# Differential attention heads: value products and norm sums in float32r halves, with the work of a head put in another order

## What is computed

```python
def diff_attention(x, w_qkv, w_o, lq1, lk1, lq2, lk2, subln_g, lambda_init):
    qkv = x @ w_qkv                      # 8 heads, two 64-wide q/k parts, v of 128
    q = apply_partial_rope(q, cos, sin) * (HEAD_DIM ** -0.5)
    k = apply_partial_rope(k, cos, sin)
    s = jnp.where(mask, jnp.einsum('bqhcd,bkhcd->bhcqk', q, k), -jnp.inf)
    p = jax.nn.softmax(s, axis=-1)
    a = p[:, :, 0] - lam * p[:, :, 1]
    o = jnp.einsum('bhqk,bkhe->bqhe', a, v)
    o = rmsnorm(o, subln_g) * (1.0 - lambda_init)
    return o.reshape(B, S, V_WIDTH) @ w_o
```

## Time and profile before

| | us |
|---|---|
| runs | 2322.46, 2322.62, 2324.59 |
| median | 2322.62 |
| profiled execution, its own time | 2322.65 |
| its span | 2320.9 |
| PE busy | 2300.4 (99%) |
| DVE busy | 1278.9 (55%) |
| ACT busy | 816.7 (35%) |
| POOL busy | 96.5 (4%) |

### The profile page before, as it was taken

How to read it: one execution, slowest core, us unless ns; L and a number is a source line. 1 busy time by engine, 2 the same in 40 slices (tenths; PEclk the granted TensorE clock), 3 DMA queues, 4 the chain that set the end, 5 groups by cost and what they waited for, 6 DMA issues and landing times.

```text
span 2320.9 us, 28961 instructions
## 1 busy us (share of the span) xinstructions
PE 2300.4 (99%) x10614; PEld 1841.6 (79%) x10614; DVE 1278.9 (55%) x1662; ACT 816.7 (35%) x1113; POOL 96.5 (4%) x82
## 2 busy tenths in 40 slices
PE   9999999999999999999999999999999999999999
PEld 8877888888865788888887777888887887888886
DVE  5453643444688644444547867454456655654553
ACT  5376532322413532322424544222224223322222
POOL 0000000000000000000003311000001001000002
PEclk9999999999999999999999999999999999999999
DMA  5210332332553233333332112332332322333331
GB/s 199 82 48 26 109 99 91 99 100 91 186 158 105 73 100 100 98 95 97 108 100 64 55 45 74 109 100 91 99 96 71 113 92 73 109 94 96 99 95 51
DMA packets 64791, 220.05 MB, mean 95 GB/s; under 512 B 8576, under 2 KB 8960, under 8 KB 64448
## 3 DMA queue, kind: packets, MB, share of 16 engines
q1 hardware_dynamic: 64704, 218.85, 30.2%
HBM read 208.62 MB, written 2.10 MB: 91 GB/s over the span
## 4 chain that ended last, share of the span: by engine, by line
PE 94%; DVE 2%; ACT 2%; issue 1%; DMA 0%; POOL 0%; SPq 0%; DVEq 0%; ACTq 0%; POOLq 0%
PE ps L1605 87%; PE ps L2005 2%; PE ps L2098 1%; PE ps L2124 1%; PE ps L1871 1%; PE ps L2114 0%; PE ps L2103 0%; PE ps L1886 0%; DVE spl L1009 0%; ACT sph L532 0%; PE ps L2131 0%; PE ps L1851 0%; PE ps L1665 0%; DVE m L870 0%; DVE sp L1004 0%
## 5 line engine op out<-in xcount | busy, mean ns | idle before, releaser
L1605 PE MATMUL ps<-xh,whi 128*128 128x512 f32 x1764 | 697.9, 396 | 1.4 <-DVE xl L845 0.8
L1605 PE MATMUL ps<-xh,wlo 128*128 128x512 f32 x1764 | 687.1, 390 | 0.0
L1605 PE MATMUL ps<-xl,whi 128*128 128x512 f32 x1764 | 686.7, 389 | 0.0
L839 DVE TENSOR_TENSOR wlo<-raw,whi 128x1024 fp32r<-128x1024 f32 x380 | 473.7, 1247 | 242.9 <-ACT whi L368 233.5
L368 ACT ACTIVATE whi<-raw 128x1024 fp32r<-128x1024 f32 x380 | 398.8, 1050 | 495.4 <-PE ps L1605 492.8
L1605 PE MATMUL ps<-yh,whi 128*128 128x512 f32 x1116 | 437.0, 392 | 1.2 <-DVE m L1375 0.8
L1605 PE MATMUL ps<-yh,wlo 128*128 128x512 f32 x1116 | 434.4, 389 | 0.0
L1605 PE MATMUL ps<-yl,whi 128*128 128x512 f32 x1116 | 434.2, 389 | 0.0
L1605 PEld LDWEIGHTS ps<-xh,whi 128*128 128x128 f32 x1764 | 331.4, 188 | 80.7 <-issue 7.1
L1605 PEld LDWEIGHTS ps<-xl,whi 128*128 128x128 f32 x1764 | 331.3, 188 | 71.5 <-issue 4.5
L1605 PEld LDWEIGHTS ps<-xh,wlo 128*128 128x128 f32 x1764 | 331.1, 188 | 69.8
(11 more groups left out here) (250 smaller groups left out, 1831.2 us busy)
## 6 DMA issues: line engine op xcount, KB each, us to landing
raw<-stream SPq DMA_DIRECT2D x380, 512.0 KB, 3.5
u<-ub SPq DMA_DIRECT2D x118, 67.0 KB, 2.4
tapw<-taps SPq DMA_DIRECT2D x1, 3584.0 KB, 12.1
h<-x_t SPq DMA_DIRECT2D x8, 256.0 KB, 6.0
raw<-stream SPq DMA_DIRECT2D x8, 256.0 KB, 6.2
out_t<-h SPq DMA_DIRECT2D x8, 256.0 KB, 2.3
const<-consts SPq DMA_DIRECT2D x1, 1089.0 KB, 9.0
vec<-vecs SPq DMA_DIRECT2D x1, 180.0 KB, 10.2
```

Source lines behind the costliest of these rows:

```text
L839: dve.tensor_tensor(wlo[:, a.slot], raw[:, a.slot], whi[:, a.slot].bitcast(F32), ALU.subtract)\
L1605: mm = pe.matmul(out, lhs, rhs, start=first and n == 0, stop=last and n == 2)
```

## The change

- v is split: ACT rounds v into vh, POOL stores vl; for the last head both go into block 7 of yh and yl. The transposed weights are split as well: ACT writes the high half into aT, DVE the low half straight from bank 6 (`turned_lo`). `values` then runs once for a head, after all four transposes, in 12 float32r passes of 512, 384, 256 and 128 columns, three of each, where it was 10 float32 matmuls (20 records).
- Bank 6 is free for the next transposes when `turned_lo` has read it (da_al), no longer when ACT has copied it (da_aT).
- The square is split too (ACT into sums 0, DVE `square_lo` into sums 1), and `norm_sum` becomes two float32r passes.
- PE issues the next head's first scores right behind the last transposes and ahead of `values`; `norm_sum` moves behind the next four blocks.
- The scaling by lambda moves from DVE to ACT (`scale`). DVE folds the norm into the tables once (sinq, sin, cos: three operations ahead of the first rotation) and `rope` is two operations, both reading the bank, where it was three. The k tile's rope moves into the following head, behind `inverse(e, 1)`; that of the last k tile stands in head 6.
- In head 6 and 7, `out_lo` stands behind the second `turned_lo`, `split_lo(T_DO + 1)` later than it did, and the last `values(1)` behind three output units.
- The table load at the head of each pair goes (4 loads). Outside the attention, semaphores are merged and nothing is moved on an engine; the copy `exact` has 768 columns, not 640.

The core of the diff: ACT, DVE, POOL, PE.

```diff
+                def scale(e, u):
+                    n, p, kv = 4 * e + u, u % 2, (u + 1) * P
+                    act.wait_ge(s("da_r1"), i * 8 + (n + 1))
+                    act.activation(A["ex"][:, p, 1, 0:kv], A["ex"][:, p, 1, 0:kv], ACT.Copy, scale=A["r1"][:, p])\
+                       .then_inc(s("da_t"), 1)
...
-                def out_square(e):
-                    act.wait_ge(s("da_o"), i * 2 + (e + 1) + CREDIT)
...
+                def stage(e):
+
+                    act.wait_ge(s("da_o"), i * 2 + e + CREDIT)
+                    act.wait_ge(evac_done, T_DA)
+                    act.activation(A["vh"][:], A["dv"][:, :, bass.ds(i * 256 + e * 128, P)], ACT.Copy).then_inc(s("da_vhh"), 1)
+
+                def stage_last():
+
+                    act.wait_ge(s("da_qn"), 2 * DA_HEADS + CREDIT)
+                    act.activation(yh[:, KB - 1].rearrange("p (t c) -> p t c", t=TB), A["dv"][:, :, D - P:D], ACT.Copy)\
+                       .then_inc(s("da_vhh"), 1)
+
+                def out_square(done):
+
+                    act.wait_ge(s("da_o"), done + CREDIT)
                     act.activation(sq[:, 0], ps[:, 7], ACT.Square).then_inc(s("da_sq"), 1)
+                    act.wait_ge(s("da_sq"), done)
+                    act.activation(sums[:, 0], sq[:, 0], ACT.Copy).then_inc(s("da_sqh"), 1)
...
-                act.preload_act_table_set(LN_EXP)
                 for e in (0, 1):
+                    last = e or before
                     exps(e, 0)
-                    if e or before:
+                    scale(e, 0)
+                    if last:
+                        out_square(i * 2 + e)
+                    exps(e, 1)
+                    if fill or e == 0:
+                        stage(e)
+                    if last:
                         out_rms(i * 2 + e)
...
                     copy_T(e, 0)
-                    if e or before:
+                    scale(e, 1)
+                    exps(e, 2)
+                    if last:
                         out_hi(i * 2 + e, i * 2 + (e - 1))
-                    exps(e, 2)
+                    if not fill and e == 0:
+                        stage_last()
+                    scale(e, 2)
...
                     exps(e, 3)
+                    scale(e, 3)
                     copy_T(e, 2)
                     copy_T(e, 3)
-                    out_square(e)
```

```diff
                 dve.wait_ge(tile_done, t.count)
                 if not isinstance(done, int) or done > 2:
                     dve.wait_ge(s("da_qn"), done - 2 + CREDIT)
-                dve.scalar_tensor_tensor(A["draw"][:, c], ps[:, c], 1.0 if c else 64 ** -0.5, rrow[:], ALU.mult,
-                                         ALU.mult).then_inc(evac_done, 1)
-                dve.wait_ge(s("lam_ready"), 2)
-                dve.wait_ge(evac_done, t.count)
-                dve.stream_shuffle(A["dsh"][:, c], A["draw"][:, c], swap).then_inc(s("da_sh"), 1)
-                dve.wait_ge(s("da_sh"), done)
-                dve.tensor_tensor(A["dsh"][:, c], A["dsh"][:, c], cst("sin"), ALU.mult).then_inc(s("da_shs"), 1)
+                straight, crossed = drow[:, c], dcross[:, c]
+                dve.wait_ge(s("da_trig"), 3)
+                dve.scalar_tensor_tensor(straight, ps[:, c], 1.0 if c else 64 ** -0.5, cst("cos"), ALU.mult, ALU.mult)
+                dve.wait_ge(s("lam_ready"), 1)
+                dve.stream_shuffle(crossed, ps[:, c], swap).then_inc(evac_done, 1)
                 if split:
                     split_lo(t)
 
...
-                def combine(e, u):
-
-                    n, p, kv = 4 * e + u, u % 2, (u + 1) * P
-                    done = i * 8 + (n + 1)
+                def inverse(e, u):
+
+                    n, p = 4 * e + u, u % 2
                     dve.wait_ge(s("da_exp"), i * 16 + 2 * (n + 1) + CREDIT)
                     dve.reciprocal(A["rc"][:, p], A["sm"][:, p]).then_inc(s("da_rcp"), 1)
-                    dve.wait_ge(s("da_rcp"), done)
+                    dve.wait_ge(s("da_rcp"), i * 8 + (n + 1))
                     dve.tensor_tensor(A["r1"][:, p], A["rc"][:, p, 1:2], nlam[:], ALU.mult).then_inc(s("da_r1"), 1)
-                    dve.wait_ge(s("da_r1"), done)
-                    dve.tensor_scalar(acc[:, 0:kv], A["ex"][:, p, 1, 0:kv], A["r1"][:, p], None, ALU.mult)\
-                       .then_inc(s("da_t"), 1)
-                    dve.wait_ge(s("da_t"), done)
+
+                def combine(e, u):
+
+                    n, p, kv = 4 * e + u, u % 2, (u + 1) * P
+                    dve.wait_ge(s("da_t"), i * 8 + (n + 1))
                     if u >= 2:
                         dve.wait_ge(s("da_T"), i * 8 + (n - 1))
                     dve.scalar_tensor_tensor(A["da"][:, p, 0:kv], A["ex"][:, p, 0, 0:kv], A["rc"][:, p, 0:1],
-                                             acc[:, 0:kv], ALU.mult, ALU.add).then_inc(s("da_a"), 1)
+                                             A["ex"][:, p, 1, 0:kv], ALU.mult, ALU.add).then_inc(s("da_a"), 1)
+
+                def turned_lo(e, u):
+
+                    dve.wait_ge(s("da_aT"), i * 8 + (4 * e + u + 1))
+                    dve.tensor_tensor(turned(1, u), turned_in(u), turned(0, u).bitcast(F32), ALU.subtract)\
+                       .then_inc(s("da_al"), 1)
...
+                def square_lo(done):
+
+                    dve.wait_ge(s("da_sqh"), done)
+                    dve.tensor_tensor(sums[:, 1], sq[:, 0], sums[:, 0].bitcast(F32), ALU.subtract).then_inc(s("da_sql"), 1)
+
                 for e in (0, 1):
+                    last = e or before
+                    filled = fill and last or e == 0 and before
                     row_max(e, 0)
                     row_max(e, 1)
+                    if filled:
+                        split_lo(Tile(T_DA + 3 + 2 * e, i))
+                    inverse(e, 0)
+                    if last:
+                        square_lo(i * 2 + e)
                     combine(e, 0)
-                    if e or before:
+                    inverse(e, 1)
+                    if filled:
+                        rope(1, Tile(T_DA + 3 + 2 * e, i), i * 4 + (2 * e + 4), False)
+                    row_max(e, 2)
+                    if last:
                         out(i * 2 + e)
-                    row_max(e, 2)
-                    if e or before:
-                        out_lo(i * 2 + e, i * 2 + (e - 1))
                     combine(e, 1)
+                    turned_lo(e, 0)
                     if not fill and e:
-                        split_lo(Tile(T_DO + 1))
                         early_sum(2)
-                    combine(e, 2)
+                    inverse(e, 2)
                     if fill:
                         rope(0, Tile(T_DA + 4 + 2 * e, i), i * 4 + (4 + 2 * e + 1), False)
                     row_max(e, 3)
+                    combine(e, 2)
+                    turned_lo(e, 1)
+                    if last:
+                        out_lo(i * 2 + e, i * 2 + (e - 1))
                     if not fill:
                         early_sum(3 * e)
+                    inverse(e, 3)
                     combine(e, 3)
+                    turned_lo(e, 2)
                     if fill:
                         split_lo(Tile(T_DA + 4 + 2 * e, i))
-                        rope(1, Tile(T_DA + 4 + 2 * e + 1, i), i * 4 + (4 + 2 * e + 2))
-                    elif e == 0:
+                    elif e:
+                        split_lo(Tile(T_DO + 1))
+                    if not fill and e == 0:
                         early_sum(1)
+                    turned_lo(e, 3)
+                    if not fill and e == 0:
                         split_lo(Tile(T_DO))
                 if not fill:
                     split_lo(Tile(T_DO + 2))
                     early_sum(4)
                     split_lo(Tile(T_DO + 3))
+                    square_lo(DA_HEADS)
                     early_sum(5)
                     out(DA_HEADS)
                     out_lo(DA_HEADS, DA_HEADS - 1)
```

```diff
+            def pair_work(pair):
                 for e in (0, 1):
+                    stage(pair, e)
                     rotated(pair, e, 0)
                     rotated(pair, e, 1)
-                    stage(pair, e)
-
-            pair_inputs(0)
-            with pool.Fori(1, 4) as pair:
-                pair_inputs(pair)
+
+            for e in (0, 1):
+                rotated(0, e, 0, 0)
+                rotated(0, e, 1, 0)
+            pair_work(0)
+            with pool.Fori(1, 3) as pair:
+                pair_work(pair)
+            stage(3, 0)
+            stage(3, 1, True)
```

```diff
                 def transposes(e, u):
                     n = 4 * e + u
                     pe.wait_ge(s("da_a"), i * 8 + (n + 1))
-                    pe.wait_ge(s("da_aT"), i * 8 + n + CREDIT)
+                    pe.wait_ge(s("da_al"), i * 8 + n + CREDIT)
...
-                def values(e, u):
-                    n, at = 4 * e + u, P * u * (u + 1) // 2
-                    pe.wait_ge(s("da_aT"), i * 8 + (n + 1) + CREDIT)
```

(50 more changed lines are left out.)

134 lines of the change are left out of this document (78 added, 56 removed).

## The result

The changed kernel takes 2327.45 us (median, 2326.01 to 2329.03), the kernel before 2323.18 on the same chips. The ratio is 1.0019, with a 95% interval of 1.0013 to 1.0024. So the change costs 4.3 us, where 3.2 us of gain were forecast, and the time lies outside the range. From the first scores to the sum behind the output projection the changed kernel takes 1413.75 - 1226.54 = 187.2 us, 182.9 before and 179.7 by the forecast. The whole loss is in this stretch.

What follows compares the result with a forecast made beforehand. PE was taken to bound the kernel (94% of the last-ending chain). Gains of 5.4, 3.7 and 2.7 make 11.8 us, less 8.6 of new waits leaves 3.2: 2322.65 to 2319.4 us, range 2316.0 to 2322.6.

Steps and rivals of the forecast that it cites:

- PE's own prices: Values from 2.61 to 1.94 us a head, norm sum from 0.92 to 0.46; over eight heads 5.4 and 3.7 us gained.
- The door: Start of head 6: the first output unit waits for the last k tile's rope, PE stands 4.8 us, bounds 4 and 5.5.
- Wait 2: Norm sum in heads with filling tiles: its chain is level with PE's work, 0 taken, up to 1.5 us.
- The wait on yl: Units 10 and 11 of head 6 need head 5's yl from the later out_lo; PE stands 1.3 us.
- the early sum: Head 6, behind the units waiting on yl: PE stands 0.2 us for the sum of the same bank.
- wait 5: Two norm sums at the end: 0.7 us of waiting in head 7 and 0.2 behind it.
- The wait ahead of the values: Each of seven heads: PE waits 0.2 us for the split of the last transposes, 1.4 us in all.
- waits that go: Exponentials in head 0 (0.9 us), an early sum in the last pair (0.8), last transposes in seven heads (1.0): 2.7 us gained.
- rival C: The norm sum's chain is late everywhere; with 1.5 us a head the time is 2328.4; chance 0.07, milder form 0.1.
- rival B: PE comes back at half rate behind head 6's 4.8 us stall, losing 2.3 us, time 2321.7; chance 0.23.
- Rival A: Head 6's wait for the last tile falls away or is short: gain 8.0 us, time 2314.6; chance 0.12.

Runs made afterwards that it cites:

- e1: Changed kernel with the first output unit of head 6 waiting for one tile fewer, not the last k tile; 2321.01 us, ratio 0.9990.
- e10: e5 with the norm sum as one float32 matmul of the square again; 2318.72 us, ratio 0.9982 to the kernel before.
- e5: Changed kernel with head 6's first output unit waiting one tile fewer, v's low half between rotations, out_lo behind third turned_lo in filling heads; 2315.87 us.
- e2: Changed kernel with POOL's rotation operations and low half of v beside the heads cut to 8 columns, for times alone; 2323.01 us, ratio 0.9998.
- e9: Changed kernel with PE running 19 more passes into empty bank 0 while it waits for the last k tile in head 6; 2325.61 us, ratio 1.0011.
- e6: Changed kernel with the scaling by lambda back from ACT to DVE, ahead of each combine; 2334.23 us, ratio 1.0047.
- e4: Changed kernel with POOL doing v's low half between the two rotations of a head instead of ahead of both; 2324.82 us, ratio 1.0008.

## Why the prediction was wrong

**What held.** PE's own prices: the values from start to start 1.98 (e1's rows, 1344.93 to 1346.91) for a forecast of 1.94, a gain of 0.63 for 0.67; the norm sum two passes of 0.23, in e10 against e5 worth 0.40 for 0.46. The door: 4.43 us of idle time, 4.6 by the starts (the distance of two starts, less the pass between them), for 4.8, at the place and for the reason that was walked through. The profile puts this wait down to "issue" and not to DVE's shuffle, but the shuffle of the last k tile runs from 1349.48 to 1350.20, PE starts at 1350.30, and e1 takes the wait away by that tile's count alone. Wait 2 on the norm sum in the heads with filling tiles, called the soft place: no wait at all, as taken. The wait on yl 1.14 of idle time, 1.31 by the starts, for 1.3; the early sum 0.20, 0.37 by the starts, for 0.2; wait 5 in head 7 0.41 for 0.7. The wait ahead of the values: from the masks to the values the starts lie 0.62 and 0.82 apart in turn, where the masks alone take 0.50, so 0.12 and 0.32 for 0.2 in each.

**What failed: "waits that go", the last transposes.** I wrote that the combine gets one block more and credited 0.15 for each of seven heads. In its place the transposes wait 0.6 to 0.75 us in heads 1 to 5, which eats nearly all that PE saves there. The credit itself was there to take in those five heads only: in heads 0 and 6 of the kernel before the last transposes start 0.24 and 0.23 behind the pass, with no wait. The sum asked for the path of DVE only at four places (values, norm sum, door, yl) and here it didn't: `transposes(e, 3)` now waits for `turned_lo(2)`, which on DVE stands behind `combine(e, 3)`, and that behind everything from the third row maximum on. With DVE at its usual durations that is just in time (e2: no wait). But DVE loses some 2.2 us a head to POOL, 0.8 at the combine, 0.5 at r, 0.75 at `out_lo` by the starts of the next operations and 0.15 at the larger combine. On PE that comes to 19.80 - 18.95 = 0.85 a head, 4.3 us in five.

The sign of it stood in the forecast's own rows. The earlier trace rows has `split_lo` at 1.77 beside POOL and 1.22 without; I used this as a bound for one chain and in rival C, and against C set that POOL should be idle "then". The question should have been asked for every DVE operation with two inputs in SBUF, since the change moves those: in the heads of the kernel before, POOL's rows lie beside shuffles, row maxima and `split_lo`, and the combines, the product with lambda and `out_lo` run while POOL is idle. The Trainium skill, "SBUF — State Buffer", section "Who interferes with whom", says that a DVE instruction with two SBUF inputs contends with a GpSimd instruction that reads SBUF, and that whichever comes first keeps the shared ports for its whole length; one with at most one such input doesn't contend unless it runs in a 2-port mode. By that rule three of DVE's operations in each head are held until POOL's operation ends, and the rows of the changed kernel and e2 agree, down to the product of one column that took 0.83 us and ended within 0.01 us of POOL's vl. It was a rule that spoke against this change, and the forecast didn't weigh it.

**What was priced, but not chosen: rival B.** The forecast gave 0.23 to PE coming back at half rate behind the door, at 2.3 us. It did, at 1.7 us in the changed kernel (e9 gives 1.55 in the trace, 1.8 by the medians). The Trainium skill, "TensorE: Matmul & The Clock Gate", Part 1, whose rule stood beside this rival, agrees with this trace: the granted clock fell behind a stall of 4.4 us in the middle of the program. It stayed at 1.00 around the wait of 1.14 (e5, 1351 to 1359), and the passes behind the waits of 0.75 come at the full rate. One reading of the earlier trace rows has to be taken with care: the profile lists a granted clock of 1.00 for 1.46 to 6.10 us as well, so there only the durations speak for 1.2 GHz, while behind the door clock and distances agree.

**Rival C** named a slower kernel by DVE's lateness, but at the wrong wait: no row waits on the norm sum in heads 1 to 5. Its price, five or six times the lateness of a head, and its reason, POOL, were close, though the `split_lo` that it named keeps its 1.22 (head 5, 1324.74). Rival A was false as it stood, and e1 made it true by one number.

**The balance.** The stretch missed by 7.5 us. Heads 1 to 5 account for 4.8: 4.3 for POOL's hold, the rest for gains of 0.63 and 0.40 instead of 0.67 and 0.46. The clock behind the door is 1.7. Head 0 is 0.5 above its part, 0.24 of it a wait for its first combine and 0.15 the credit for a wait that wasn't there. Head 6 has 24.9 us by the forecast's terms (19.72 before, less 0.67, 0.46 and 0.15, plus 0.2, 4.8 and 1.5) and took 26.93: beyond the clock 0.3 more, as the door gives back 0.2, the start behind each of the two waits on output units costs 0.1, the early sum 0.2 more by its starts, and the credit 0.15. Behind head 6 only 0.2 is missed: the sum at the end waits 0.48 for acc (L1625), which no step had, and the waits on the norm sums, 0.41 for 0.9, give it back.

## What to carry to other kernels

When an edit makes the bounding engine faster, every engine close behind it must be walked through at each wait, not only at the waits that the edit adds: saved work turns into waiting at the first place where another engine is late, and the repair of such places can be worth more than the edit (here 0.85 us in each steady head, where the edit alone gained 0.12). When an edit moves operations of DVE or POOL in time, list which DVE operations have two inputs in SBUF and what POOL runs beside them; a tiny operation ahead of a chain is as exposed as a large one. A counter that stands for "all tiles are out" is a wait for the last one: ask which one is needed; and price a stall of some us on PE with the slow clock behind it.

## What the runs showed of the hardware

- DVE held by POOL: 1.26, 0.83 and 1.44 us for operations of 0.48, 0.16 and 0.68, ending 0.28, 0.01 and 0.56 us behind POOL's operation. Operations with an input in a bank kept their time (0.74, 0.28). POOL's operation is also somewhat longer when DVE has begun first (1.48 for 1.29).
- An in-place scaling with a single SBUF tensor as input was held too, in e6: 0.96 us for 256 columns beside POOL in head 5, 0.35 in head 6 with POOL idle.
- The granted clock fell to 0.50 within or just behind a stall of 4.4 us and came back 3.7 us after work began in the trace of the changed kernel, 5 us after in that of e4. That a mean clock of 0.999 for the execution hides 1.7 us was new to me; windows of 1 us show it.
